# Two feed-forward up projections with the weight tile stationary and the turned activations moving

## The reference

```python
h  = rms_norm(x, gain)                  # 256 x 2048
u  = h @ w_up                           # 2048 x 11264 (gate half and value half, 5632 each)
u  = depthwise convolution of width 3 over the tokens, per channel
g, v = split(u)
x  = x + rms_norm((act(g) * v) @ w_down, gain2)   # 5632 x 2048
```

## Time and profile before

| | |
|---|---|
| median of three runs | 2851.84 us |
| lowest, highest run | 2845.36, 2853.04 us |
| span of the profiled execution, first to last instruction | 2842.9 us |
| PE busy | 2662.4 us, 94% |
| DVE busy | 1666.0 us, 59% |
| ACT busy | 1347.8 us, 47% |
| POOL busy | 414.8 us, 15% |
| mean granted clock of PE | 0.956 |

### The profile page before, as it was taken

One profiled execution on the slowest core, in us unless ns is written; L12 is line 12 of the kernel. 1 busy time (PEld: TensorE's weight loads), 2 busy tenths in 40 slices (PEclk: granted clock), 3 DMA queues, 4 the chain that ended last, 5 costly groups with the idle time before them and its releaser, 6 DMA issues.

```text
span 2842.9 us, 38254 instructions
## 1 busy us (share of the span) xinstructions
PE 2662.4 (94%) x13482; PEld 2128.7 (75%) x13482; DVE 1666.0 (59%) x1810; ACT 1347.8 (47%) x1778; POOL 414.8 (15%) x228
## 2 busy tenths in 40 slices
PE   7899789999999999999979798986999999999998
PEld 6688557788888887887858586765778888887886
DVE  4443754566666665445494857667466666665444
ACT  4443643466555554434524242433465555554333
POOL 1000000011212121000070605143002112121000
PEclk9999957999999999999999898998999999999999
DMA  8866303566666566565535354542646666666664
GB/s 198 234 190 177 119 23 94 158 182 181 182 179 181 180 177 198 180 194 175 165 112 173 108 157 121 156 125 92 189 149 179 183 183 174 185 177 198 189 187 140
DMA packets 242451, 465.11 MB, mean 164 GB/s; under 512 B 14328, under 2 KB 23329, under 8 KB 241841
## 3 DMA queue, kind: packets, MB, share of 16 engines
q1 hardware_dynamic: 240001, 453.44, 53.0%
q0 software_dynamic: 2240, 10.28, 1.8%
q10 hardware_dynamic: 112, 0.03, 0.0%
HBM read 458.46 MB, written 5.23 MB: 163 GB/s over the span
## 4 chain that ended last, share of the span: by engine, by line
PE 84%; DVE 8%; issue 3%; ACT 2%; DMA 2%; POOL 1%; DVEq 0%; SPq 0%; ACTq 0%; POOLq 0%
PE acc L225 26%; PE acc L226 26%; PE acc L227 26%; DVE wlo L212 3%; DMA raw<-in_w_in_dram 2%; PE tp L464 1%; DVE qd L1430 1%; PE tp L270 1%; PE tp L962 1%; DVE ib L1421 1%; PE acc L926 1%; ACT whi L207 1%; PE tp L1289 1%; PE tp L943 0%; DVE pf L1420 0%
## 5 line engine op out<-in xcount | busy, mean ns | idle before, releaser
L212 DVE TENSOR_TENSOR wlo<-raw,whi 128x1024 fp32r<-128x1024 f32 x856 | 1190.7, 1405 | 980.9 <-ACT whi L207 979.4
L207 ACT ACTIVATE whi<-raw 128x1024 fp32r<-128x1024 f32 x856 | 901.4, 1059 | 1152.2 <-PE acc L227 1011.0
L225 PE MATMUL acc<-whi,ahi 128*128 128x512 f32 x2656 | 1073.8, 404 | 77.4 <-DVE wlo L212 62.5
L226 PE MATMUL acc<-wlo,ahi 128*128 128x512 f32 x2656 | 1061.6, 400 | 0.0
L227 PE MATMUL acc<-whi,alo 128*128 128x512 f32 x2656 | 1060.3, 399 | 0.0
L225 PEld LDWEIGHTS acc<-whi,ahi 128*128 128x128 f32 x2656 | 506.5, 191 | 207.3 <-DVE wlo L212 74.9
L227 PEld LDWEIGHTS acc<-whi,alo 128*128 128x128 f32 x2656 | 505.4, 190 | 124.3
L226 PEld LDWEIGHTS acc<-wlo,ahi 128*128 128x128 f32 x2656 | 506.6, 191 | 118.3
L225 PE MATMUL acc<-whi,hhi 128*128 128x512 f32 x704 | 278.2, 395 | 0.0
L226 PE MATMUL acc<-wlo,hhi 128*128 128x512 f32 x704 | 278.1, 395 | 0.0
L227 PE MATMUL acc<-whi,hlo 128*128 128x512 f32 x704 | 278.1, 395 | 0.0
(11 more groups left out here) (209 smaller groups left out, 1555.0 us busy)
## 6 DMA issues: line engine op xcount, KB each, us to landing
raw<-in_w_up_dram SPq DMA_DIRECT2D x176, 512.0 KB, 3.8
raw<-in_ffn_w_in_dram SPq DMA_DIRECT2D x176, 512.0 KB, 4.1
raw<-in_hgrn_w_in_dram SPq DMA_DIRECT2D x160, 512.0 KB, 3.8
raw<-in_w_in_dram SPq DMA_DIRECT2D x88, 512.0 KB, 3.6
raw<-in_w_down_dram SPq DMA_DIRECT2D x88, 512.0 KB, 4.5
raw<-in_ffn_w_out_dram SPq DMA_DIRECT2D x88, 512.0 KB, 4.6
raw<-in_w_out_dram SPq DMA_DIRECT2D x32, 512.0 KB, 4.2
raw<-in_hgrn_w_out_dram SPq DMA_DIRECT2D x32, 512.0 KB, 4.5
```

The lines of the kernel that those rows point to most:

```text
L207: act.activation(whi[:, s, :], raw[:, s, :], ACT.Copy).then_inc(hi_done, 1)
L212: dve.tensor_tensor(wlo[:, s, :], raw[:, s, :], whi[:, s, :].bitcast(F32), ALU.subtract).then_inc(lo_done, 1)
L225: pe.matmul(out[:, t, :], xh, whi[:, s, c], start=(kt == 0), stop=False)
L226: pe.matmul(out[:, t, :], xh, wlo[:, s, c], start=False, stop=False)
```

## The change

- `products_turned` takes the place of `products` in both up stages. For each k tile there are four channel tiles of 128 (`ct`); the weight tile is stationary and the 256 tokens of `ahi` or `alo` move. The product comes out with channels on the partitions.
- `turn` is gone from PE, and so are `utok` and the semaphores around it.
- `evacuate` moves from ACT to DVE: one instruction for a whole half of 1024 elements, `acc` times a row `rowr` that holds the norm's factor of each of the 256 tokens. It lies behind the split of chunk 3 (of the value half before) and of chunk 11 (of the gate half).
- The row is made once in each stage: two DVE instructions make diagonal matrices (`row_scale`), PE multiplies them with a matrix of ones into `tp[0]` (one float32 matmul of 256 columns behind chunk 9), and DVE copies it out.
- `centre` and `convolve` read `ut` in SBUF where they read `tp` in PSUM.

```diff
+        def products_turned(pe, n, s, out, k0, ready=None):
+            pe.wait_ge(lo_done, n + 1)
+            o = out[:, :, :].rearrange("p n c -> p (n c)")
+            for k in range(CK):
+                kt = k0 + k
+                if ready:
+                    pe.wait_ge(sem("pre_lo"), lo_ready(ready, kt))
+                for ct in range(4):
+                    c, d = slice(k * GC + ct * P, k * GC + (ct + 1) * P), slice(ct * S, (ct + 1) * S)
+                    pe.matmul(o[:, d], whi[:, s, c], ahi[:, kt, :], start=(kt == 0 and ct % 2 == 0), stop=False,
+                              skip_group_check=True)
+                    pe.matmul(o[:, d], whi[:, s, c], alo[:, kt, :], start=False, stop=False, skip_group_check=True)
+                    mm = pe.matmul(o[:, d], wlo[:, s, c], ahi[:, kt, :], start=False, stop=(kt == KT - 1),
+                                   skip_group_check=True)
+            mm.then_inc(chunk_used, 1)
...
         def up_pe(pe, ph, src_ready):
-            def turn(i, half):
-                pe.wait_ge(group_free, gb[ph] + half + 1 + i * 2)
-                for k in range(4):
-                    for t in range(NT):
-                        mm = pe.transpose(tp[half][:, k, t * P:(t + 1) * P], utok[half][:, t, k * P:(k + 1) * P],
-                                          ident[:, :])
-                mm.then_inc(sem(f"{ph}_uturned{half}"), 1)
...
-                    products(pe, cb[ph] + c + i * BODY, c % RING, acc[(gb[ph] + c // CPG) % 2], ahi, alo,
-                             CK * (c % CPG), KT, ph if first and c < CPG else None)
-                    if c == 1 and not first:
-                        turn(i - 1, 1)
-                    if c == CPG + 1:
-                        turn(i, 0)
+                    products_turned(pe, cb[ph] + c + i * BODY, c % RING, acc[(gb[ph] + c // CPG) % 2],
+                                    CK * (c % CPG), ph if first and c < CPG else None)
+                    if first and c == CPG + 1:
+                        pe.wait_ge(sem(f"{ph}_diag"), NT)
+                        pe.wait_ge(sem("ones"), 1)
+                        pe.matmul(tp[0][:, 0, :], ones[:, :], cvu[:, 0, :], start=True, stop=True)\
+                          .then_inc(sem(f"{ph}_row"), 1)
...
-            turn(FG - 1, 1)
...
         def up_dve(dve, ph, b, source):
+            def evacuate(i, half):
+                dve.wait_ge(chunk_used, cb[ph] + CPG * (half + 1) + i * BODY)
+                if half or not isinstance(i, int) or i:
+                    dve.wait_ge(sem(f"{ph}_conv{half}"), i * 8 + 8 * half)
+                dve.tensor_tensor(ut[half][:, :, :],
+                                  acc[(gb[ph] + half) % 2][:, :, :].rearrange("p n (k c) -> p (n k) c", c=S),
+                                  bcast(rowr[:, :], 1, 4), ALU.mult).then_inc(group_free, 1)
...
-                        dve.scalar_tensor_tensor(out=cv[half][:, k, o], in0=tp[half][:, k, u],
+                        dve.scalar_tensor_tensor(out=cv[half][:, k, o], in0=ut[half][:, k, u],
...
+            def row_scale():
+                dve.wait_ge(sem(f"{ph}_rstd"), 1)
+                for t in range(NT):
+                    dve.tensor_scalar(cvu[:, 0, t * P:(t + 1) * P], ident[:, :], rstd[:, 2 * b + 1, t:t + 1], None,
+                                      ALU.mult).then_inc(sem(f"{ph}_diag"), 1)
...
                     if c == 7 and first:
                         sumsq_dve(dve, ph, 2 * b + 1)
+                        dve.memset(edge[:, :], 0.0).then_inc(sem(f"{ph}_conv1"), 8)
+                        row_scale()
+                    if c == 3 and not first:
+                        evacuate(i - 1, 1)
...
+                    if c == CPG + 3:
+                        if first:
+                            dve.wait_ge(sem(f"{ph}_row"), 1)
+                            dve.tensor_copy(rowr[:, :], tp[0][:, 0, :]).then_inc(sem(f"{ph}_row"), 1)
+                            dve.wait_ge(sem(f"{ph}_row"), 2)
+                        evacuate(i, 0)
...
             for c in range(LEAD):
                 s_lo(dve, f"down{b + 1}", 0, 0, c)
+            evacuate(FG - 1, 1)
             convolve(FG - 1, 1)
```

More of the change, by code:

```diff
@@ L82, in bass_two_blocks @@
         prime = sb("prime", [P, 1])
+        rowr = sb("rowr", [P, S])
+        ones = sb("ones", [P, P])
+        edge = sb("edge", [P, 1])
         psq = sb("psq", [P, 4, NT, NG])
@@ L91, in bass_two_blocks @@
         with ExitStack() as r:
-            utok = [sb(f"utok{j}", [P, NT, GC], where=r) for j in range(2)]
+            ut = [sb(f"ut{j}", [P, 4, S], where=r) for j in range(2)]
             cvg = sb("cvg", [P, 4, S], where=r)
@@ L482, in up_pe @@
                 body(i, False)
-            turn(FG - 1, 1)
         def up_act(act, ph, b, x_sem, x_count):
             cv = (cvg, cvu)
[L488 to L493, removed]
             def centre(i, half):
-                act.wait_ge(sem(f"{ph}_uturned{half}"), i + 1)
+                act.wait_ge(group_free, gb[ph] + half + 1 + i * 2)
                 act.wait_ge(sem(f"{ph}_hid"), i + 1)
@@ L500, in centre @@
                     ct = i * 4 + (half * FT + k)
-                    act.activation(cv[half][:, k, :], tp[half][:, k, :], ACT.Identity,
+                    act.activation(cv[half][:, k, :], ut[half][:, k, :], ACT.Identity,
                                    bias=taps[:, b, 3, bass.ds(ct, 1)],
@@ L516, in body @@
                         nonlinear(i - 1)
-                    if c == 3 and not first:
-                        evacuate(i - 1, 1)
                     if c == 7 and first:
@@ L522, in body @@
                         centre(i - 1, 1)
-                    if c == CPG + 3:
-                        if first:
-                            act.wait_ge(sem(f"{ph}_rstd"), 1)
-                        evacuate(i, 0)
                     if c == CPG + 5:
@@ L534, in up_act @@
                 s_hi(act, f"down{b + 1}", 0, 0, c)
-            evacuate(FG - 1, 1)
             centre(FG - 1, 1)
@@ L545, in convolve @@
                     if j:
-                        dve.wait_ge(sem(f"{ph}_conv{half}"), i * 8 + 4)
+                        dve.wait_ge(sem(f"{ph}_conv{half}"), i * 8 + 4 + 8 * half)
                     o = slice(d, S) if d > 0 else slice(0, S + d)
@@ L577, in up_pool @@
                 pool.wait_ge(sem(f"{ph}_nl"), i + 1)
-                pool.wait_ge(sem(f"{ph}_conv1"), i * 8 + 8)
+                pool.wait_ge(sem(f"{ph}_conv1"), i * 8 + 16)
                 pool.tensor_tensor(cvg[:, :, :], cvg[:, :, :], cvu[:, :, :], ALU.mult).then_inc(sem(f"{ph}_pr"), 1)
@@ L637, in setup_pool @@
                 pool.dma_start(lam4[:, j, :], bcast(T[name][0], 0, P)).then_inc(mix_in, 16)
+            pool.memset(ones[:, :], 1.0).then_inc(sem("ones"), 1)
             pool.wait_ge(sem("toep"), 1)
```

## The result

The change makes the kernel faster: 2804.45 us, median of four runs (2799.76 to 2809.37), against 2848.87 (2845.36 to 2853.04) for the kernel before beside it. The ratio is 0.9845 with a 95% interval of 0.9827 to 0.9863, some 44 us less. The span of the profiled execution falls by 45.0 us, from 2842.9 to 2797.9.

What follows compares the result with a forecast made beforehand. PE was taken as the bound, up-stage time being its instructions times their pace. Terms -38.6 - 3.1 + 0.2 + 4.6 + 0.9 = -36.0 us took 2851.84 to 2815.8 us; range 2806 to 2836.

Steps and rivals of the forecast that it cites:

- The transposes: Up stages: PE's eight transposes per half go, 44 turns at 0.877 us, 38.6 us off the path.
- The idle time at the stage's end: End of each up stage: PE's wait for ACT's last evacuation goes, 1.56 us a stage, 3.1 us off.
- the +0.2 of a late hand-over: Start of each down stage: 0.1 us of new PE wait, +0.2 us; bounds nothing and 1.5 us a stage.
- The larger of 117.2 and 111.7 is 117.2, and I take that.: Up stages: a 256-column matmul takes 117.2 ns with full loads hidden, +4.6 us; bounds 116.65 and 118.0 ns.
- Row of factors: Each up stage: one float32 matmul of 256 columns, 0.44 us, +0.9 us for both; bounds nothing and 2 us.
- DVE's evacuation: Up stages: 1.23 us on DVE, 44 times, 54 us more DVE work, hidden in its idle time.
- the reads from SBUF: `centre` and `convolve`: eight operations at 476 ns may become some per cent slower or faster, hidden.
- Rival (a): Up stages: each load costs PE 20 ns however short the matmul, 126.7 ns each, 2896 us; chance 0.08.
- Rival (b): Up stages: load and matmul cost each other 1.5 to 3.5 ns, 13 to 30 us, 2829 to 2846; chance 0.08.
- (c): Up stages: weight loads not hidden, +598 or +1588 us, about 3414 or 4400 us; chance 0.02.
- (d): Up loop: PE's instructions come too slowly, refetching the longer body costs 60 us, 2876 us; chance 0.02.
- (e): Hand-over or each half: DVE or ACT late, up to 3 or 10 us, 2817 to 2828; inside the range.

Runs made afterwards that it cites:

- Experiments 2: Changed kernel with 32 unused bytes per partition ahead of `psq`, so activations start 32 bytes further on (288 from the weights); 2812.23 us, ratio 0.9861.
- 6: Changed kernel with a second pair of activation tiles for the up stages, 32 bytes further on (288), elsewhere 256; 2776.16 us, ratio 0.9745.
- 12: Changed kernel with 480 unused bytes ahead of `psq`, restoring the activations' old distance from the weights (224); 2825.01 us, ratio 0.9903.
- the sweep: Kernel before, then changed kernel, each with activations at a different distance from the weights in various stages; 2840.91 and 2817.93 us.
- experiment 1: Kernel before with 32 unused bytes per partition ahead of `psq`, putting the activations at 256 from the weights instead of 224; 2787.44 us, ratio 0.978.
- experiment 11: Changed kernel loading 64 instead of 128 weight columns per matmul in the up stages, half the channels left out; 2801.37 us.
- Experiment 10: Changed kernel with activation tiles placed per stage, `ahi` / `alo` at 384 / 128 in `up1` and 260 / 4 in `up2`; 2817.93 us.
- Experiment 7: Kernel before with `ahi` at 256 from the weights, `alo` alone 32 bytes further at 288, `hhi` and `hlo` at 384; 2847.39 us.

## Why the prediction missed, step by step

The sign and the working of the parts held; one term was mis-sized and one was missing. The two errors have opposite signs: the pace cost 23.7 us more than forecast, and the untouched stages gave 31.8 that nobody had forecast. That the forecast of 2815.8 came within 11.4 us of 2804.45 is luck.

- **The transposes, -38.6.** Right. No transpose of the product is left, and with the layout held the up stages fall by 26.3 us. The terms with the pace measured there are -38.6 - 3.1 + 0.9 + (8448 x 118.33 ns = 999.7, less 985.5 = +14.2) = -26.6.
- **The idle time at the stage's end, -3.1, and the +0.2 of a late hand-over.** The first is right; the second was nothing. The first products of `down1` follow at ordinary distances.
- **"The larger of 117.2 and 111.7 is 117.2, and I take that."** This is the term that was mis-sized. At the place where the change put the activations, the matmul takes 120.0 ns: 8448 x 120.0 = 1013.8 us, +28.3 instead of +4.6. The bounds of 116.65 and 118.0 did not hold it. The gate sums and L1289 were read as the price of a shape. Experiments 2, 6 and 12 and the sweep show one shape with one load at 116.7, 118.3, 118.7, 120.0 and 123.3 ns, so neither row could give it; the gate sums themselves went to 115.9 with the change, while the turned products stood at 120.0. With 120.0 the up stages' terms sum to -38.6 - 3.1 + 0.9 + 28.3 = -12.5 us; -13.1 was measured.
- **No term for the stages that are not touched.** This is the term that was missing, and the one that carried the time out of the range. The diff has three lines with new tiles, and I gave them no cost. They moved the activations from d = 224 to 256, and 31.8 us came off stages whose code did not change. That placement does this is shown by experiment 1, where it is the only edit, and by its reverse in 12. Together -12.5 - 31.8 = -44.3, of the 45.0 measured in the span. With the places held (12) the time is 2825.0, inside the stated range and 9.2 over the likeliest value, and the pace accounts for that: +14.2 instead of +4.6.
- **Row of factors, DVE's evacuation, the reads from SBUF.** Right: 0.43 us, 1218 ns, 478 ns, and PE without idle time in the loop. The DMA share rose from 0.61 to 0.62.
- **Rival (a), 20 ns for each load however short the matmul.** Its time is far off, yet half of its idea is seen. At d = 256 both forms stand 13.3 ns over their columns (226.7 over 213.3; 120.0 over 106.7), a fixed sum for each matmul. At d = 288 the excess goes with the columns instead (20.0 over 213.3, 10.0 over 106.7). My argument against (a), that the excess goes with the columns, was made from rows at other places and does not hold at 256. At 121.5 ns the gain would have been gone, and the stage at 260 / 4 passes that point.
- **Rival (b), 1.5 to 3.5 ns that load and matmul cost each other.** The size was met (2.8 ns over 117.2), but whether this is what load and matmul cost each other stays open: half the load's width changed nothing in the loop and took 6.7 ns off in the first ten chunks (experiment 11), and the distance of the tiles alone moved the pace by 6.6. Its time was not met, since the untouched stages gave more than it cost.
- **Rivals (c), (d), (e).** None came. Loads of 188 ns lie beside matmuls 116.7 ns apart on the same rows of the array (192 and 120.0 in the changed kernel). The Trainium skill, "TensorE: Matmul & The Clock Gate", Part 3, "What overlaps and what doesn't", has weight loads overlap with matmuls in flight only when the row group differs; the trace does not agree with it here either.

Was the change good, then? By the runs at equal d: at 224 it gains 27 us (2851.9 to 2825.0); at 256 it loses 17 (2787.4 to 2804.5), of which 13.7 lie in the up stages. At 288, with the other stages at 233.3 ns as before, it gains some 40 (2812.2). The 44 us measured are a small gain in the up stages and a larger one from 1568 bytes that nobody meant. With each form at its own place it is worth having: 2776.2 us, 11 below the kernel before with its own best pad that was run.

## What to carry to other kernels

Read a diff for what it allocates, too: new tiles ahead of TensorE's operands shift them against each other. Here that was worth up to 64 us of 2850, more than the change under study. Before crediting an edit, time it with the tiles' places held (with a pad that restores the old difference), and look first at the pace of matmuls that the edit did not touch. Read paces stretch by stretch: a mean over the whole stage hides that experiment 11 has two, 113.3 and 120.0 ns. Where TensorE is the bound, try a few pads, and try them for each form of matmul by itself.

## What the hardware showed that was not expected

- The pace of `fp32r` matmuls depends on where the moving and the stationary tile start relative to each other: 226.7 to 234.2 ns for 512 columns, 116.7 to 123.3 for 256, at the full clock, with no idle time on PE and full overlap of the loads. Moving both tiles together by 32 bytes changed nothing for these products; the gate sums went from 117.2 to 115.9 ns when both their tiles moved by 32.
- The best place for one form is not the best for the other: 256 is fast for 512 columns (226.7) and poor for 256 (120.0); 288 is slow for the first (233.3) and the best seen for the second (116.7).
- A kernel's earlier matmuls can matter: with loads of 64 columns at d = 256 the turned products start every 113.3 ns, and from one float32 matmul on every 120.0 ns until the stage ends. The cause is not shown.
- The law stays open. Two simple ones, a period of 64 bytes and "only multiples of 256 are fast", fell in the sweep: 384 is a multiple of 64 and slow (233.3), 192 and 448 lie between (228.9). Experiment 10 does not separate `ahi` from `alo`: its 123.3 (260 / 4) and 118.7 (384 / 128) have the two tiles at different d. Experiment 7 shows that a neighbouring matmul's operand enters as well. No run looks at what in the memory or in TensorE does this, and the two forms were tried with the same d for both tiles only at 224, 256 and 288.
